# A hybrid transformer block on one core: two of four depthwise-convolution tiles made by GpSimd beside the first attention, and two projection units instead of four

## The reference, cut to what matters

```python
u = rmsnorm(h, g_mix[i])
z = u @ w_in[i]
zq, zkv, zg, zc, zm = jnp.split(z, IN_SPLITS, axis=-1)
kv = ...                                   # 6 tensors of 2 groups x 64 features
kc = compress(kv[0], cmp_pos_k[i], w_cmp_k1[i], w_cmp_k2[i])   # 31 blocks of 32 positions, stride 16
vc = compress(kv[1], cmp_pos_v[i], w_cmp_v1[i], w_cmp_v2[i])
o_c, o_s, o_w = nsa_attention(q, kc, vc, kv[2], kv[3], kv[4], kv[5])
c_val, c_gate = jnp.split(zc, 2, axis=-1)
c = c_val * jax.nn.sigmoid(c_gate)         # 512 channels
c = causal_dwconv(c, conv_w[i], conv_b[i]) # 31 taps a channel
c = jax.nn.silu(layernorm(c, conv_ln_g[i], conv_ln_b[i]))
```

## Time and profile before

| | |
|---|---|
| median of three runs | 2157.8 us (2157.7 to 2158.95) |
| profiled execution | 2159.29 us, span 2157.5 us |
| granted TensorE clock | 0.998 of full speed |
| busy: TensorE / VectorE / ScalarE / GpSimd | 2127.7 / 1006.3 / 879.4 / 936.5 us |
| matmuls | 10070 |
| first attention | about 125 to 322 us |

### The profile page before, as it was taken

How to read it: one execution, slowest core, us unless ns; L and a number is a source line. 1 busy time by engine, 2 the same in 40 slices (tenths; PEclk the granted TensorE clock), 3 DMA queues, 4 the chain that set the end, 5 groups by cost and what they waited for, 6 DMA issues and landing times.

```text
span 2157.5 us, 25220 instructions
## 1 busy us (share of the span) xinstructions
PE 2127.7 (99%) x10070; PEld 1739.1 (81%) x10070; DVE 1006.3 (47%) x1790; ACT 879.4 (41%) x1365; POOL 936.5 (43%) x424
## 2 busy tenths in 40 slices
PE   9999999999999999999999999999999999999998
PEld 7877778888888887777778888888888888888886
DVE  5887865265525235666635322314633254223134
ACT  5444455344424254555434422324522244223234
POOL 5632124444444455222235444445544454444446
PEclk9999999999999999999999999999999999999999
DMA  4421113333333332211122333332223323333322
GB/s 161 147 87 41 49 50 98 94 102 98 98 98 98 97 109 79 69 51 57 50 88 79 97 98 98 98 97 87 90 92 96 96 79 98 97 98 98 98 86 80
DMA packets 53829, 193.26 MB, mean 90 GB/s; under 512 B 6096, under 2 KB 6224, under 8 KB 53712
## 3 DMA queue, kind: packets, MB, share of 16 engines
q1 hardware_dynamic: 52992, 189.81, 28.3%
q10 hardware_dynamic: 720, 1.84, 0.3%
HBM read 189.53 MB, written 2.10 MB: 89 GB/s over the span
## 4 chain that ended last, share of the span: by engine, by line
PE 90%; DVE 5%; ACT 4%; issue 1%; POOL 0%; DMA 0%; DVEq 0%; ACTq 0%; POOLq 0%
PE ps L518 28%; PE ps L520 27%; PE ps L519 27%; PE ps L730 1%; ACT w_hi L1862 1%; PE ps L983 1%; PE ps L1002 1%; PE ps L722 1%; PE ps L712 1%; PE ps L614 1%; PE ps L1009 1%; DVE xg_lo L1173 1%; PE ps L1011 0%; PE ps L1010 0%; ACT fprob L2001 0%
## 5 line engine op out<-in xcount | busy, mean ns | idle before, releaser
L471 POOL TENSOR_TENSOR w_lo<-w_raw,w_hi 128x1024 fp32r<-128x1024 f32 x352 | 854.2, 2428 | 1182.6 <-ACT w_hi L1862 1182.5
L518 PE MATMUL ps<-xg_hi,w_hi 128*128 128x512 f32 x1688 | 675.1, 400 | 4.9 <-POOL w_lo L485 2.6
L520 PE MATMUL ps<-xg_hi,w_lo 128*128 128x512 f32 x1688 | 659.4, 391 | 0.0
L519 PE MATMUL ps<-xg_lo,w_hi 128*128 128x512 f32 x1688 | 658.7, 390 | 0.0
L1862 ACT ACTIVATE w_hi<-w_raw 128x1024 fp32r<-128x1024 f32 x352 | 372.0, 1057 | 626.1 <-PE ps L520 623.0
L518 PEld LDWEIGHTS ps<-xg_hi,w_hi 128*128 128x128 f32 x1688 | 317.6, 188 | 79.6 <-issue 12.4
L520 PEld LDWEIGHTS ps<-xg_hi,w_lo 128*128 128x128 f32 x1688 | 317.4, 188 | 68.0
L519 PEld LDWEIGHTS ps<-xg_lo,w_hi 128*128 128x128 f32 x1688 | 318.0, 188 | 59.6
L518 PE MATMUL ps<-h_hi,w_hi 128*128 128x512 f32 x688 | 267.6, 389 | 0.0
L519 PE MATMUL ps<-h_lo,w_hi 128*128 128x512 f32 x688 | 267.6, 389 | 0.0
L520 PE MATMUL ps<-h_hi,w_lo 128*128 128x512 f32 x688 | 267.6, 389 | 0.0
(11 more groups left out here) (342 smaller groups left out, 2425.3 us busy)
## 6 DMA issues: line engine op xcount, KB each, us to landing
w_raw<-in_weights SPq DMA_DIRECT2D x352, 512.0 KB, 3.5
out_x<-mixed SPq DMA_DIRECT2D x8, 256.0 KB, 2.1
resid<-in_x SPq DMA_DIRECT2D x3, 512.0 KB, 7.9
p_raw<-in_p ACTq DMA_DIRECT2D x3, 512.0 KB, 3.5
resid<-in_x SPq DMA_DIRECT2D x2, 256.0 KB, 4.2
last_gain<-in_last_gain SPq DMA_DIRECT2D x1, 512.0 KB, 4.4
w_raw<-in_weights SPq DMA_DIRECT2D x1, 256.0 KB, 3.6
w_raw<-in_weights ACTq DMA_DIRECT2D x1, 256.0 KB, 3.8
```

Source lines behind the costliest of these rows:

```text
L471: pool.tensor_tensor(w_lo[:, slot, :], w_raw[:, u % RAW, :], w_hi[:, slot, :].bitcast(F32), ALU.subtract).then_inc(w_ready, 1)
L518: pe.matmul(o, w, x, start=start, stop=False)
L519: pe.matmul(o, w, xl, start=False, stop=False)
L520: return pe.matmul(o, wl, x, start=False, stop=stop)
```

## The change

`cmp_in` has two units instead of four: one for the keys, one for the values, each with both groups' 64 columns once. VectorE makes the four doubled tiles out of them, again by eight instructions, now reading either half of the partitions for both halves. The group still has five units, now with three of `glu`. The first key unit (`key0`) moves forward, behind the last of the first four `glu` units; the two last hidden units of the values stand next to each other. Banks, waits and the order on VectorE and ScalarE follow.

Of the convolution VectorE makes tiles 0 and 3, all taps within the attention, two a step as before; none stand ahead of it. GpSimd makes tiles 1 and 2: after each of the splits of the first 16 "pairs" units four taps, each of them a product with the weight into a buffer and an addition to `conv_acc` (the first of a tile is one instruction). The additions to `ln_sum` stand at (4,1), (7,3) and (7,3).

```diff
-    stage("cmp_in", 4)
+    stage("cmp_in", 2)
     stage("glu", 4)
+    stage("key0", 1)
     stage("hidden_k", 8)
-    stage("hidden_v", 8)
+    stage("hidden_v", 7)
...
-            bank[glu_unit(t)] = (4, 5, 6, 0, 1, 2, 3, 0)[t]
+            bank[glu_unit(t)] = (4, 5, 6, 2, 3, 0, 1, 2)[t]
...
-            bank[kv_unit(n)] = (1, 2, 3, 0)[n]
+            bank[kv_unit(n)] = (1, 3, 0, 1)[n]
...
-EARLY_TAPS = 62
+DVE_TILES, POOL_TILES = (0, 3), (1, 2)
-LN_ADD = ((0, 1), (4, 0), (7, 3))
+LN_ADD = {(4, 1): (1,), (7, 3): (2, 3)}
...
+            pool_tapped = [0]
+
+            def taps(count):
+
+                if pool_tapped[0] == 0:
+                    pool.wait_ge(s_kv["turned"], 2)
+                    pool.wait_ge(vec_loaded, 16)
+                    pool.wait_ge(bank_free, glu_unit(2 * POOL_TILES[-1] + 1) + 1)
+                for n in range(pool_tapped[0], min(pool_tapped[0] + count, len(POOL_TILES) * CONV_TAPS)):
+                    ct, k = POOL_TILES[n // CONV_TAPS], n % CONV_TAPS
+                    acc, src, w = conv_acc[:, ct, :], glu[:, ct, k:k + S], vcol("conv_w", ct * CONV_TAPS + k)
+                    if k == 0:
+                        pool.tensor_scalar(acc, src, w, vcol("conv_b", ct), ALU.mult, ALU.add).then_inc(s_mrg["pconv"], 1)
+                    else:
+                        product = T2[:, n % 2, :]
+                        if n > 2:
+                            pool.wait_ge(s_mrg["pconv"], n - 1)
+                        pool.tensor_scalar(product, src, w, None, ALU.mult, ALU.bypass).then_inc(s_mrg["tap"], 1)
+                        pool.wait_ge(s_mrg["tap"], n - n // CONV_TAPS)
+                        pool.wait_ge(s_mrg["pconv"], n)
+                        pool.tensor_tensor(acc, acc, product, ALU.add).then_inc(s_mrg["pconv"], 1)
+                pool_tapped[0] += count
...
                     low(u)
+                    if U["pairs"] <= u < U["pairs"] + 16:
+                        taps(4)
...
-            for t in range(1, 4):
-                unit(glu_unit(t))
+            unit(glu_unit(3))
+            unit(kv_unit(0))
             for i in range(4):
                 hidden(0, i)
                 unit(glu_unit(4 + i))
-            for n in range(4):
-                hidden(1, n)
-                unit(kv_unit(n))
-                if n == 0:
-                    hidden_turn(0)
+            hidden(1, 0)
+            unit(kv_unit(1))
+            hidden_turn(0)
+            hidden(1, 1)
+            unit(kv_unit(2))
+            hidden(1, 2)
+            hidden(1, 3)
+            unit(kv_unit(3))
             hidden_turn(1)
...
-            for j in range(4):
-                uu = U["cmp_in"] + j
+            for kv in range(2):
+                uu = U["cmp_in"] + kv
                 dve.wait_ge(unit_done, uu + 1)
-                dve.tensor_tensor(kv_dup[0:HD, j, :], ps[0:HD, BANK[uu], :], R[0:HD, 0, :], ALU.mult).then_inc(s_cmp["dup"], 1)
-                dve.tensor_tensor(kv_dup[HD:P, j, 0:S - 1], ps[HD:P, BANK[uu], 1:S], R[HD:P, 0, 1:S], ALU.mult).then_inc(bank_free, 1)
+                for g in range(2):
+                    rows = slice(g * HD, (g + 1) * HD)
+                    dve.tensor_tensor(kv_dup[0:HD, 2 * kv + g, :], ps[rows, BANK[uu], :], R[rows, 0, :], ALU.mult).then_inc(s_cmp["dup"], 1)
+                    dve.tensor_tensor(kv_dup[HD:P, 2 * kv + g, 0:S - 1], ps[rows, BANK[uu], 1:S], R[rows, 0, 1:S],
+                                      ALU.mult).then_inc(bank_free if g else s_cmp["dup"], 1)
...
             blocks(0, "pos_k")
             glu_tile(0)
+            block_low(0)
             blocks(1, "pos_v")
-            block_low(0)
             dve.wait_ge(bank_free, glu_unit(1) + 1)
-            taps(2)
             block_low(1)
             glu_tile(1)
-            taps(14)
+            dve.wait_ge(bank_free, glu_unit(3) + 1)
+            keys(0)
...
-            highs(glu_unit(0) + 1 + RING)
-            highs(glu_unit(1) + 1 + RING)
+            highs(glu_unit(2) + 1 + RING)
             block_high(0)
             glu_sigmoid(0)
-            highs(glu_unit(2) + 1 + RING)
+            highs(kv_unit(0) + 1 + RING)
             block_high(1)
```

More of the change, by code:

```diff
@@ L93, in hidden_unit @@
 def hidden_unit(kv, i):
-    return layout_units()[("hidden_k", "hidden_v")[kv]] + 2 * i
+    U = layout_units()
+    return U["hidden_v"] + (0, 2, 4, 5)[i] if kv else U["hidden_k"] + 2 * i
 def kv_unit(n):
-    return layout_units()["hidden_v"] + 2 * n + 1
+    U = layout_units()
+    return U["hidden_v"] + (1, 3, 6)[n - 1] if n else U["key0"]
 def merge_unit(m):
@@ L131, in bank_table @@
     bank = {}
-    for i in range(4):
+    for i in range(2):
         bank[U["cmp_in"] + i] = i
     for t in range(8):
-        bank[glu_unit(t)] = (4, 5, 6, 0, 1, 2, 3, 0)[t]
+        bank[glu_unit(t)] = (4, 5, 6, 2, 3, 0, 1, 2)[t]
     for n in range(4):
-        bank[kv_unit(n)] = (1, 2, 3, 0)[n]
+        bank[kv_unit(n)] = (1, 3, 0, 1)[n]
     bank[U["q0"]], bank[U["gates"]] = 2, 0
@@ L367, in build @@
         s_gate = stage_sems("gate", "sig", "turned", "ready")
-        s_mrg = stage_sems("merge", "sig", "conv")
+        s_mrg = stage_sems("merge", "sig", "conv", "tap", "pconv")
         s_ln = stage_sems("ln", "sum", "mean", "cent", "sq", "acc", "var", "sd", "inv", "bc", "n", "act", "hi", "lo")
@@ L1247, in kv_scaled @@
                 dve.wait_ge(unit_done, kv_unit(n) + 1)
-                dve.tensor_tensor(out, bank(kv_unit(n)), R[:], ALU.mult).then_inc(bank_free, 2)
+                dve.tensor_tensor(out, bank(kv_unit(n)), R[:], ALU.mult).then_inc(bank_free, (1, 2, 2, 3)[n])
             def keys(j):
@@ L1262, in _ @@
             dve.wait_ge(s_glu["pad"], 1)
-            for j in range(4):
-                uu = U["cmp_in"] + j
+            for kv in range(2):
+                uu = U["cmp_in"] + kv
                 dve.wait_ge(unit_done, uu + 1)
-                dve.tensor_tensor(kv_dup[0:HD, j, :], ps[0:HD, BANK[uu], :], R[0:HD, 0, :], ALU.mult).then_inc(s_cmp["dup"], 1)
-                dve.tensor_tensor(kv_dup[HD:P, j, 0:S - 1], ps[HD:P, BANK[uu], 1:S], R[HD:P, 0, 1:S], ALU.mult).then_inc(bank_free, 1)
+                for g in range(2):
[3 more added lines that the diff above has]
+                                      ALU.mult).then_inc(bank_free if g else s_cmp["dup"], 1)
             for t in (kc_hi, kc_lo):
                 dve.tensor_scalar(t[:, NC1:NCP], ones[:, 0:1], 0.0, None, ALU.mult).then_inc(s_cmp["out"], 1)
-            dve.wait_ge(s_cmp["dup"], 4)
-            dve.wait_ge(bank_free, U["cmp_in"] + 4)
+            dve.wait_ge(s_cmp["dup"], 6)
+            dve.wait_ge(bank_free, U["cmp_in"] + 2)
             blocks(0, "pos_k")
             glu_tile(0)
+            block_low(0)
             blocks(1, "pos_v")
-            block_low(0)
             dve.wait_ge(bank_free, glu_unit(1) + 1)
-            taps(2)
             block_low(1)
             glu_tile(1)
-            taps(14)
+            dve.wait_ge(bank_free, glu_unit(3) + 1)
+            keys(0)
+            dve.wait_ge(bank_free, kv_unit(0) + 1)
+            dve.wait_ge(s_kv["lo"], 1)
             glu_tile(2)
-            taps(14)
             dve.wait_ge(bank_free, glu_unit(5) + 1)
             glu_tile(3)
-            taps(4)
-            keys(0)
             hidden_low(0)
-            taps(6)
+            dve.wait_ge(bank_free, glu_unit(7) + 1)
             keys(1)
-            taps(8)
             dve.wait_ge(bank_free, kv_unit(1) + 1)
             kv_scaled(2, T2[:, 0:1, :])
-            taps(8)
             kv_scaled(3, T2[:, 1:2, :])
@@ L1305, in _ @@
             values_low(0)
-            taps(EARLY_TAPS - 56)
             query_scaled(0)
@@ L1416, in ln_add @@
             def ln_add(ct):
-                dve.wait_ge(s_mrg["conv"], (ct + 1) * CONV_TAPS)
+                for tile in (0, 1) if ct == 1 else (ct,):
+                    if tile in DVE_TILES:
+                        dve.wait_ge(s_mrg["conv"], (DVE_TILES.index(tile) + 1) * CONV_TAPS)
+                    else:
+                        dve.wait_ge(s_mrg["pconv"], (POOL_TILES.index(tile) + 1) * CONV_TAPS)
                 if ct > 1:
@@ L1457, in _ @@
                         head_low(A1, event(b) + i, i)
[L1458 removed]
+                    if tapped[0] < len(DVE_TILES) * CONV_TAPS:
                         taps(1)
@@ L1461, in _ @@
                         cmp_peak(p + 1)
-                    if (j, i) in LN_ADD:
-                        ln_add(LN_ADD.index((j, i)) + 1)
+                    for ct in LN_ADD.get((j, i), ()):
+                        ln_add(ct)
                     if j == 8 and i == 0:
@@ L1951, in values_high @@
                     copy_hi(vv_hi[:, hd, j, :, cols], ps[:, 3, :].rearrange("p (a b) -> p a b", b=P)[:, :, cols], s_kv["hi"])
-            highs(glu_unit(0) + 1 + RING)
-            highs(glu_unit(1) + 1 + RING)
+            highs(glu_unit(2) + 1 + RING)
             block_high(0)
             glu_sigmoid(0)
```

(17 more changed lines are left out.)

6 lines of the change are left out of this document (3 added, 3 removed).

## The result

The changed kernel takes 2196.3 us (median of 4 runs, 2195.3 to 2200.8), the kernel before 2158.2 us measured with it: 1.018 times as long, 95% interval 1.0163 to 1.0198. The forecast of 2177 us had the direction, but a growth of 19 us where 38 came, and it named VectorE as the engine that would bound the attention, where GpSimd did. The profiled execution took 2195.3 us, with a span of 2193.5.

The account below looks back on a forecast made before the run. TensorE, busy 99% of the span, was taken to bound the kernel, with VectorE bounding the changed attention. Span 2157.5 - 9.4 (front) + 28 (attention) = 2176.1 us, median forecast 2177 us, range 2149 to 2208 us.

Parts of the forecast that it names:

- Parts 1 and 2, the front: Ahead of the attention: two projection units fewer save 10.9 us, new order costs 1.5 us; attention starts 9.4 us earlier.
- the one for `blk_lo`: In the front: TensorE's first hidden unit waits 0.5 us for the blocks' low part, bounds 0 and 1.5 us.
- The one near the end: Late in the front: TensorE waits 1 us for the last value unit's weight split, bounds 0 and 1.5 us.
- Part 3, no taps ahead: Ahead of the attention: VectorE loses 62 taps, 46 us; gives nothing, as TensorE didn't wait for VectorE there.
- Part 4, the product at 0.7 us: In the attention: GpSimd makes 62 taps with a one-input product of 0.7 us; a tap takes 2.6 us.
- the formula of the forecast: GpSimd in the attention: first split's end, fifteen units of 12.9 us and two taps give 310.4 us, +22 us.
- The rival of the dear product: GpSimd's product costs 1.28 us like the sum, a unit 15.3 us; net +50 us, 2207 us; chance 0.15.
- The port: In the attention: VectorE waits for GpSimd at the shared port, 1.5 us a pair, 48 us, plus 8 us on the compressed branch.
- The slack: In the attention: VectorE's 27.8 us of idle time absorbs part of its 56 us of added work, leaving +28 us.
- Half of each: Rival: the attention grows by 5 to 13.7 us, some 2158 us, no change; chance 0.08.
- the faster case: Rival: VectorE's slack takes all port waits, 22 us; net -9.4 to -5.8 us, 2148 to 2152 us; chance 0.20.

Follow-up runs that it names:

- old_front: The changed kernel with the earlier front (four compression units, old order); GpSimd still makes tiles 1 and 2 with the same taps: 2204.1 us.
- front_only: The changed kernel with all four convolution tiles on VectorE, 62 taps ahead of the attention, none on GpSimd: 2162.7 us.
- prod_add0: The changed kernel with GpSimd's product written as times the weight plus 0.0, same values: 2168.5 us.
- one_tile: The changed kernel with one tile on GpSimd, two taps behind each split, and three on VectorE, 31 taps ahead: ratio 1.0015 to the kernel before.
- one_tile_add0: one_tile with the product written as times the weight plus 0.0: ratio 1.0001 to the kernel before.
- one_tile_late: one_tile_add0 with the taps from the third to the eighteenth attention unit, no gates: ratio 0.9984 to the kernel before.
- sums_only: The changed kernel without GpSimd's products; it adds the shifted input unweighted: ratio 1.0030 to the kernel before.

## Why the prediction was right or wrong, step by step

**Parts 1 and 2, the front: right.** Forecast 9.4 us, measured 9.1. The attention starts at 115.6 us as forecast; the first `blk_lo` was ready at 48.6 us instead of 49.7. Of the two waits that I forecast, the one for `blk_lo` (0.5 us) didn't come, as TensorE got to it at 49.3; two waits for `w_lo`, 1.7 us by 70 us, came that I hadn't. The one near the end was 0.8 us, where 1 was forecast. It is 7.9 us in the medians of old_front and after.

**Part 3, no taps ahead: right as it stood, incomplete.** TensorE didn't wait for VectorE there, and I read from it that their going gives nothing. front_only shows that with the shorter front it is worth the whole 9 us. A row could have told it: VectorE had 73.1 us of work in the 84 of the front, and a front 9.4 us shorter leaves 74.6, so 1.5 us for all of VectorE's own waits. Out of the old front, the taps were worth 1.3 us (old_front begins the attention at 123.4 instead of 124.7).

**Part 4, the product at 0.7 us: the step that failed.** The bounds were 0.53 (MEMSET) and 1.28 us (a sum of two inputs). It took 1.56 us, outside both: I argued from the number of reads, and a left-out operation costs more than a present one. So GpSimd's unit was 13.9 us, not 12.9, and GpSimd, which I had 6 us under VectorE's growth and so left out of the sum, set the length. By the formula of the forecast with the measured prices, 111.7 + 15 x 13.9 + 5.8 = 326 us is when the addition of tile 2 may start, not 310.4. GpSimd's last tap ended at 327.4, and the addition started at 332.9. The miss in the unit would have been larger, had two other terms of the tap not been too high: the handovers, 0.2 us forecast and some 0.1 measured, and GpSimd held up by VectorE, 0.45 forecast and 0.08 measured (means of 1.61 and 1.30 against 1.56 and 1.27 undisturbed). With the cheap product (prod_add0) the last tap ended at 288.2. (The sum itself has a slip: 2157.8 + 18.6 is 2176.4, not 2177.) The rival of the dear product had its mechanism (TensorE waits for `w_lo` in 12 attention units) and nearly its time: 2207 against 2196 us.

The Trainium skill ("GPSIMD Engine Reference", Engine selection) calls one-input work on GpSimd roughly line-rate. By the rows, 0.72 us for 512 elements a partition is near it (VectorE's own taps of that width take 0.75), 1.56 is not, and the page doesn't tell the two forms apart.

**The port: right in mechanism, too large in size.** Forecast 1.5 us a pair, 48 us in all, and 8 us on the compressed branch. Measured 26.7 us on the pairs and 1.3 on the branch (21.5 and 4.4 in prod_add0). Two reasons for the pairs show in the traces. First, the slow product lets VectorE in and the quick one doesn't. Two pairs of 128x128, of the changed kernel and of prod_add0, with GpSimd's product at that time; undisturbed such a pair takes 0.60 us:

```profile
141.50 1.57 POOL L508 TENSOR_SCALAR tile_b<-glu,vec 128x512 f32<-128x512 f32 x1
...
142.00 0.60 DVE L1384 TENSOR_SCALAR prob_w<-prob_w,stat,gates 128x128 f32<-128x128 f32 x2
...
164.98 0.69 POOL L508 TENSOR_SCALAR tile_b<-glu,vec 128x512 f32<-128x512 f32 x1
...
165.02 0.97 DVE L1384 TENSOR_SCALAR prob_s<-prob_s,stat,gates 128x128 f32<-128x128 f32 x2
```

The first lies wholly inside the slow product and loses nothing; the second loses 0.37 us to the quick one. Counted one by one over all kernels, for the instructions of the pairs that began inside one of GpSimd's and at least 0.06 us before its end: inside a quick product none of 74 ended before it, inside a sum none of 123, inside a split none of 31, and mostly they ended 0.08 us (128 wide) to 0.28 us (512 wide) behind it. Inside a slow product 58 of 87 ended before it did and lost at most 0.39 us, all between 0.86 and 0.46 us before its end, as if it let VectorE in once, in the middle. Of the 19 pairs of the changed kernel that began inside one, 11 lost at most 0.3 us; the other 8 met the sum behind it and lost 1.0 to 1.3; the mean was 0.57. The 5 that began inside a sum lost 1.13 and the 6 inside a split 1.11 (the last pair, below, apart). My price let every instruction block alike. Second, with the cheap product GpSimd is done sooner, and 7 of the 32 pairs of prod_add0 begin while it does nothing and lose nothing. The rule in the Trainium skill ("SBUF — State Buffer", Who interferes with whom: whichever engine has the shared port keeps it for its instruction) agrees with the splits, the sums and the quick product here, but not with the slow one.

**The slack: wrong.** I took 27.8 us of VectorE's idle time off the port waits. The three kernels with one ungated tile, whose clock stayed at 1.00, show what came through: one_tile +12.6 us on the 64 and +9.9 in length, one_tile_add0 +10.2 and +6.9, one_tile_late +9.7 and +4.6, so a half to four fifths. A reason that fits, not tested by itself: the idle time of the earlier trace rows is waiting for the step's own chain, and the waiting pair stands in that chain. In sums_only and prod_add0 (+21.5 and +19.1) nine tenths came through, part of it as work at a lower clock, which the forecast had at nothing: 7.0 of the 19.1 us in prod_add0, 14.4 of the 45.8 in the changed kernel. These errors and the too-large price partly cancelled, which is luck: with the product at its forecast price (prod_add0) the attention grew by 19.1 us, forecast 28.

**The end, not foreseen.** GpSimd is behind by three splits when its taps end, and VectorE's last instructions meet them:

```profile
327.37 7.44 POOL L474 TENSOR_TENSOR w_lo<-w_raw,w_hi 128x1024 fp32r<-128x1024 f32 x3
...
329.43 3.18 DVE L1384 TENSOR_SCALAR prob_w<-prob_w,stat,gates 128x512 f32<-128x512 f32 x2
332.86 3.29 DVE L1456 TENSOR_TENSOR ln_sum<-ln_sum,conv_acc 128x512 f32<-128x512 f32 x2
```

The pair takes 3.18 us instead of 1.00 and the two additions 3.29 instead of 1.36, which is 4.1 us; TensorE waits 3.3 us for the second.

**Half of each, and the faster case.** The slack doesn't take all, so the faster rival fell. The time of "half of each" is reached by another kernel, one tile with a cheap product: 2159.2 us.

## What to carry to other kernels

Before work goes to an idle engine, one instruction of exactly the form it will use must be in a trace: a bound from "fewer operands" isn't a bound. An engine that shares a port with another is best given work in the gaps of the other's chain, and only as much as leaves it idle time: a wait on the neighbour's semaphore in front of each piece kept 64 instructions at 27.0 us, where without it they took 35.3, and did nothing with two tiles, where the engine was nearly full (48.0 against 47.1 us). And a wait of zero says only that a piece of work costs nothing in the present order; what a shorter neighbour needs must be counted anew.

## What the runs showed of the hardware that was not expected

- GpSimd's `tensor_scalar` of 128x512 in float32 with a single multiplication took 1.56 us; with + 0.0 or x 1.0 behind it 0.69 to 0.72. A sum of two inputs took 1.27 to 1.30.
- VectorE's `tensor_scalar` got in beside that slow product (58 of 87 ended before it did), and never beside a quick product, a sum or a split (none of 228).
- TensorE's clock: it was 1.00 throughout the attention before. In the changed kernel it was 0.94 on average from 112 to 327 us, down to 0.83 over 20 us where TensorE waited for splits; in front_only it was 0.50, which is 1.2 GHz, from 125 to 130 us behind the stop of 5.7 us. Part of what a wait costs is therefore paid behind it: 4.8 us of longer work in front_only, and 14.4 of the 45.8 us in the changed kernel.
